# Down weights of the experts loaded through a second DMA queue, issued by ScalarE

## The reference

```
g = argmax(lg); top_v, top_i = top_k(le_g, 2)      # 1 group of 4, 2 experts of its 8
expert = g * 8 + top_i
hidden = silu(x_blk @ w_gate[e]) * (x_blk @ w_up[e])   # 1024 -> 512, twice
y_blk  = hidden @ w_down[e]                            # 512 -> 1024
out[token] += weight * y
```

## Time and profile before

| what | us |
|---|---|
| median of 3 runs (lowest, highest) | 2975.8 (2970.79, 2976.24) |
| the profiled execution | 2971.97 |
| its span, first to last instruction | 2970.1 |
| experts of layer 0, first gate product to end of last down product | 713.5 to 1198.0 |
| experts of layer 1, last down product begins | 2089.0 |
| mean granted clock of TensorE over the span | 0.937 of full speed |

### The profile page before, as it was taken

The page is one execution under the profiler, slowest core; times in us unless marked ns, Lnnn a source line. Parts: engine busy times, 40 slices in busy tenths (PEclk is TensorE's granted clock), DMA queues, the critical chain, the costliest instruction groups (busy, mean ns, idle before and its releaser), DMA issues. The chain is left out here.

```text
span 2970.1 us, 30580 instructions
## 1 busy us (share of the span) xinstructions
PE 2450.8 (83%) x11973; PEld 1304.7 (44%) x11973; DVE 983.7 (33%) x2152; ACT 550.3 (19%) x1220; POOL 166.4 (6%) x273
## 2 busy tenths in 40 slices
PE   6999888784977777497984987777498687999999
PEld 2444366443644333244743653433243553444444
DVE  3211277644222222366734222222264443001000
ACT  3000177220100000014710100000022541000000
POOL 0000000001211111000000211111000000000000
PEclk9999999886999999798996999999799788999999
DMA  8454200507999999510055999999600111221210
GB/s 303 163 192 170 73 1 1 208 30 298 418 419 419 419 418 401 192 43 19 2 193 229 417 418 418 418 418 414 221 32 0 50 72 68 102 85 59 82 57 28
DMA packets 126863, 591.81 MB, mean 199 GB/s; under 512 B 21460, under 2 KB 24028, under 8 KB 71424
## 3 DMA queue, kind: packets, MB, share of 16 engines
q1 hardware_dynamic: 116160, 568.83, 48.3%
q0 software_dynamic: 10560, 21.01, 1.9%
HBM read 579.19 MB, written 24.22 MB: 203 GB/s over the span
## 5 line engine op out<-in xcount | busy, mean ns | idle before, releaser
L1605 PE MATMUL moe_down<-moe_wd,moe_hid_t 128*64 128x512 f32 x1024 | 240.6, 612 | 62.9 <-DMA moe_wd<-in_moe_w_down 50.4
L1579 PE MATMUL moe_up<-moe_wu,moe_xg_t 128*64 128x256 f32 x2048 | 238.1, 385 | 63.2 <-DMA moe_wu<-in_moe_w_up 63.2
L1579 PE MATMUL moe_gate<-moe_wg,moe_xg_t 128*64 128x256 f32 x2048 | 239.5, 387 | 54.4 <-DMA moe_wg<-in_moe_w_gate 52.7
L395 PE MATMUL qkv_acc<-qkv_w,a_buffer 128*128 128x512 f32 x576 | 256.3, 598 | 1.4 <-DVE a_buffer L470 1.2
L2632 PE MATMUL mlp_acc<-m_h,mlp_w 128*128 128x512 f32 x512 | 224.3, 599 | 11.5 <-DMA mlp_w<-in_w_up 9.5
L1579 PEld LDWEIGHTS moe_gate<-moe_wg,moe_xg_t 128*64 128x64 f32 x2048 | 154.1, 139 | 162.0 <-DMA moe_wg<-in_moe_w_gate 91.0
L2647 PE MATMUL mlp_acc<-mlp_w,mlp_u_t 128*128 128x512 f32 x512 | 220.0, 592 | 1.4 <-DVE mlp_u_t L2667 1.4
L1579 PEld LDWEIGHTS moe_up<-moe_wu,moe_xg_t 128*64 128x64 f32 x2048 | 152.9, 138 | 144.5 <-DMA moe_wu<-in_moe_w_up 83.6
L395 PEld LDWEIGHTS qkv_acc<-qkv_w,a_buffer 128*128 128x128 f32 x576 | 107.4, 191 | 132.8 <-issue 124.0
L2632 PEld LDWEIGHTS mlp_acc<-m_h,mlp_w 128*128 128x128 f32 x512 | 97.5, 192 | 137.8 <-issue 127.9
L1665 DVE COPY moe_y<-moe_down 128x512 f32<-128x512 f32 x64 | 44.3, 692 | 342.2 <-PE moe_down L1605 342.2
(11 more groups left out here) (356 smaller groups left out, 2770.0 us busy)
## 6 DMA issues: line engine op xcount, KB each, us to landing
moe_wg<-in_moe_w_gate SPq DMA_DIRECT2D x64, 2048.0 KB, 35.1
moe_wu<-in_moe_w_up SPq DMA_DIRECT2D x64, 2048.0 KB, 34.9
moe_wd<-in_moe_w_down SPq DMA_DIRECT2D x64, 2048.0 KB, 34.9
qkv_mod_w<-in_mod_w SPq DMA_DIRECT2D x48, 1024.0 KB, 5.0
mlp_w<-in_w_up SPq DMA_DIRECT2D x8, 2048.0 KB, 8.6
mlp_w<-in_w_down SPq DMA_DIRECT2D x8, 2048.0 KB, 7.7
qkv_w<-in_a_w_qkv SPq DMA_DIRECT2D x12, 1024.0 KB, 9.5
in_w<-in_w_in SPq DMA_DIRECT2D x4, 2048.0 KB, 19.0
```

What stands on the lines that cost most here:

```text
L395: mm = nc.tensor.matmul(acc[i % 4][:], h_t[:, k, t * P:(t + 1) * P], w[:, c % w_ring, k, :], start=(k == 0), stop=(k == KD - 1))
L1579: mm = nc.tensor.matmul(acc[b][halves[f], 0:HF], xg_t[b][:, k, c, :], w[:, c, k, f * HF:(f + 1) * HF], start=(c, k) == (0, 0), stop=(c, k) ...
L1605: mm = nc.tensor.matmul(down[b][halves[c], :], hid_t[:, k, h, :], wd[z][:, 2 * h + k, c * NCHUNK:(c + 1) * NCHUNK], start=(k, h) == (0, 0) ...
```

## The change

SP no longer loads the down weights of experts 3 to 31. ACT does, in its own queue, after its work for block i and after a wait for `downed` of block i-1: it then fills the slot that block i-1 has left, with the down weights of expert i+2. The loads of experts 0 to 2 stay where they were, and so do those of blocks beyond 32, by SP.

```diff
         @block.sync
         def _(sp):
-            def refill(done, b, x):
+            def refill_first(done, b, x):
                 sp.wait_ge(s["gated"], done)
                 load_gate(sp, e, layer, ring, b, x)
                 sp.wait_ge(s["upped"], done)
                 load_up(sp, e, layer, ring, b, x)
+
+            def refill(done, b, x):
+                refill_first(done, b, x)
                 sp.wait_ge(s["downed"], done)
                 load_down(sp, e, layer, ring, b, x)
 
             for i in range(RING, NE):
-                refill(i - RING + 1, i % RING, i)
+                refill_first(i - RING + 1, i % RING, i)
...
             read_x(0, 0)
             for i in range(NE):
                 one_block(i, i % 2, i >= 1)
+                j = i - 1 + RING
+                if i >= 1 and j < NE:
+                    act.wait_ge(s["downed"], i)
+                    load_down(act, e, layer, ring, j % RING, j)
```

## The result

| | before | after |
|---|---|---|
| median of 5 runs, us | 2975.8 (2970.79 to 2979.58) | 2995.07 (2989.97 to 2999.75) |
| profiled execution, us | 2971.97 | 2989.97 |
| its span, us | 2970.1 | 2988.1 |

The changed kernel is slower by 0.6%: ratio 1.0064, 95% interval 1.0046 to 1.0082.

The account below looks back on a forecast made before the run. The prediction took the experts to be bound by weight transfers. Its terms, 7.6 us a layer and 15.2 in all, gave 2987.2 us from the profiled execution; with the runs' median 2991, it chose 2989, range 2974 to 3005.

Parts of the forecast that it names:

- The sum: Both expert layers: 1.4 + 5.37 + 0.8 = 7.6 us lost in each, 15.2 us in all, bounds 10.8 and 18.2.
- Transfers bound the experts, and the bytes end when they did: Expert phases: loads set the pace at 5.44 us each, and each layer's last bytes land when they did before.
- SyncE's stall is worth nothing: SP's issues: losing 29 a layer, 4.66 us each in the median, gains nothing, since the engines had work throughout.
- ScalarE's issues are free: ACT's 29 added issues a layer: about 0.4 us each, hidden before the next exponential, which comes 9.4 us after the copy.
- Rival 4: ACT is held in its issues, 10 us and more for each load: 3020 us or more; chance 0.04.
- The hole at the start, 1.4 us: Start of each layer: the late first down load leaves the slowest DMA engine idle 1.4 us, bounds 0 and 2.3.
- Queues served in turn, so up lands last: 5.37 us bare: End of each layer: up weights land last, leaving up product, turns and copy uncovered before the down product, 5.37 us more.
- PE is 0.8 us late: End of each layer: the last two up loads land closer than PE takes them, costing 0.8 us, bounds 0 and 1.4.
- Some 3 us of wait before each up product: Sign in the expert phases: idle time before up products grows to some 3 us each.
- 1: Rival, expert phases: two queues let the engines move more, 425 GB/s or more, giving 2962 us; chance 0.09.
- 2: Rival, end of each layer: down stays last, only the gap at the start remains, 2975 to 2979 us; chance 0.17.
- 3: Rival: the down queue gets less than a third, so down is late, 15 us a layer, 3002 to 3006; chance 0.08.

Follow-up runs that it names:

- again: The changed kernel run once more, unchanged, beside new runs of the kernel before: 2993.63 us, ratio 1.0059.
- e_swap: The kernel before, one queue, with SyncE issuing the down weights of expert 31 ahead of its up weights: 2992.39 us, ratio 1.006.
- e_early: The changed kernel, but ScalarE issues each down load after its own block's down product, as early as SyncE did before: 2988.22 us, ratio 1.0052.
- e_late1q: The kernel before, one queue, SyncE issuing all loads but each down load as late as in the changed kernel: 2990.71 us, ratio 1.0073.
- e_last2: The changed kernel with down loads issued as early as before, those of experts 30 and 31 by SyncE in the old order: 2976.64 us, ratio 1.0005.
- e_warm: e_swap, with PE repeating the gate product of block 31 twice into an unused tile while it waits: 2984.36 us, ratio 1.0033.
- e_last: The changed kernel, but SyncE issues the down weights of expert 31 again, behind its up weights: 2982.34 us, ratio 1.0034.
- e_swap_b: e_swap once more, unchanged, beside the same runs of the kernel before as e_warm: 2990.94 us, ratio 1.0065.

## Why the prediction was right

The sum was +15.2 us, and the forecast of 2989 lies 17.0 us over the profiled execution of the kernel before and 13.2 over its median; measured are +18.0 and +19.3. In the expert phases, which the sum is about, it is +16.5 and +15.7. Sign, mechanism and the larger part of the size held. That the sum came so close is partly luck: its smallest term was far off in one layer, and the two layers lost 9.8 and 6.7 us where each was given 7.6. Point by point:

- **Transfers bound the experts, and the bytes end when they did.** Held. The share is 1.01 at 418 or 419 GB/s in both kernels, and in layer 1 the last up product begins 1.3 us (again: 0.4 us) after the time of the last down product before. In e_swap, without the hole, the difference in layer 0 is 0.06 us. The prediction took the 0.58 us of the earlier trace rows for a wait; it is what a down product has with nothing missing, so in layer 1 the end of the bytes is known to about 1 us only.
- **SyncE's stall is worth nothing.** Held: its issues of up weights fell from 5.42 us in the median to 0.37, and the rate stayed.
- **ScalarE's issues are free.** Held: 0.37 us each, the lower bound. Rival 4 has no row that speaks for it.
- **The hole at the start, 1.4 us.** Held: 1.4 us by the share of one stretch of 4 us, 2.0 by its bytes, both under the upper bound of 2.3. What it costs in time isn't isolated: without it (e_early) one layer got shorter and the other longer.
- **Queues served in turn, so up lands last: 5.37 us bare.** Held. In layer 1 it can be read off: 2107.14 - 2101.78 = 5.36 us. In the second profile, and in e_early, the last up product waited for nothing: PE was still busy with what a wait one or two blocks before had left over. So the bare work is a lower bound, and the wait that decides can lie further back. That the order of the loads is the cause, and not the queue, is shown by e_swap and e_late1q, which have the loss with one queue, and by e_last2, which hasn't with two. The Trainium skill's round of the queues ("DMA: Bandwidth & Descriptors", section "Queues, rings and completion order") agrees with the row of the tile in its direction: 16.0 us to landing, not 34.9. It isn't a half share to the letter: 10.9 us of transfer and the 1.3 us to begin make 12.2, and I had named 10 to 14 us as the sign.
- **PE is 0.8 us late.** This is the term that was mis-sized. In layer 1 of the first profile it was 0. In layer 0, take the end of the bytes before, 480.8 us after the first gate product, and add the hole: 482.2, or 1196.6 in the times of the kernel after. The last up product began at 1199.76, so PE was 3.1 us late. The parts 1.4 + 5.4 + 3.1 = 9.9 us for layer 0 (measured 9.8) and 1.3 + 5.4 + 0 = 6.7 for layer 1 (measured 6.7) must add up, since the 3.1 and the 1.3 are worked out as what is left; they are no check of each other. What bears the 3.1 out by itself is the stretches of 1 us: the last weight bytes moved from 1195 to 1196, which is 3.8 to 4.8 us before PE began their product; in the kernel before, the last ones moved from 1193 to 1194, 0.3 to 1.3 us before the last down product began.
- **Why 3.1 and not 0.8.** I let a product cost the same after any wait. The up product before it had waited, worked at a clock of 0.50 for most of its time and took 2.7 us longer, and what was left to transfer no longer hid it. Without these 2.7 us the last up product would have begun at about 1197.1, 0.4 us after 1196.6. In e_warm, keeping PE busy over such a wait makes the product behind it as short as any; for this place of the changed kernel itself it wasn't tried.
- **Some 3 us of wait before each up product.** Wrong in form. It is every second one, and long, three rows of the middle:

```profile
1004.99 3.65 PE L1582 MATMUL moe_up<-moe_wu,moe_xg_t 128*64 128x256 f32 x32
...
1022.41 5.66 PE L1582 MATMUL moe_up<-moe_wu,moe_xg_t 128*64 128x256 f32 x32 [4.98 <-DMA moe_wu<-in_moe_w_up]
...
1036.66 3.65 PE L1582 MATMUL moe_up<-moe_wu,moe_xg_t 128*64 128x256 f32 x32
```

That is how the clock got low at all: before, the waits were 1.14 to 1.33 us in the steady expert, and the mean of an up matmul 385 ns. What makes the waits come in twos is open. A guess: two blocks in a row release two down loads in a row, which slow the up loads behind them; no run here takes that apart.

- **The rivals.** 1: 419 GB/s, not the 425 that I had named as its sign. 2: nobody waits for down at the end. 3: down is never late. None of them happened, and by e_last2 the second queue neither costs nor brings anything in the phases: -0.1 us, in one profile.
- **Signs that failed.** A down load took 16.0 us to land, not 10 to 14. In layer 0 PE doesn't wait for the last up weights, and the last up product begins 485.4 us after the first gate product, 4.5 us later than the last down product did; both are the lateness of PE.

**What stays open.** The medians are 19.3 and 19.9 us apart, the expert phases 16.5 and 15.7. Some three or four more microseconds lie outside, where no instruction changed, if the one profile of the kernel before stands for its runs. The outside of the twelve profiled executions runs from 2010.3 (the kernel before) to 2024.5 us (e_last, in an execution of 2993.91 us where the others of this kernel took 2979.51 to 2983.96) and follows no edit that I can name. The same excess of medians over phases, 2.0 to 5.2 us, is in all the kernels of the first two sets, and hardly in those of the last (e_warm -0.1, e_swap_b 0.7). With one profile of the kernel before, I can't say whether it is chance.

## What to carry to other kernels

Where a phase is bound by transfers, the time of its transfers is fixed, and what can still be won or lost is at its two ends: how long the DMA engines are idle before the first load, and how much work stands behind the last wait for one. So look which load lands last before splitting a queue. Here the second queue moved its loads ahead of the others (16.0 us to landing for 34.9) and so put another one last. Look also at the waits before it: after a long one PE is late and can be slow, and near the end of the phase no transfer hides that. Here it was enough to issue the down loads as early as before and to leave those of the last two experts in the order of use (e_last2): the rest went through the second queue at no cost in the phases, and at no gain.

## What the runs showed of the hardware that I had not expected

A wait of PE can cost more than its length when no transfer covers it. After 6.91 us of waiting the granted clock stood at 0.50, and a product of 3.67 us took 6.18 (2.5 us more); after 6.62 us in layer 1 of the same kernel 5.63. In e_swap_b the two products took 5.96 and 6.13 us. Filling that wait with 64 useless matmuls a layer made the expert phases 5.5 to 5.8 us shorter, 4.5 to 4.8 of them by these products. In the middle of the phase the busy time of the up products rose from 238.1 us to 278.0 in the changed kernel; in e_last2 it is 273.3, and its phases are as short as before.
